# Norms as a factor on the projections' results: a transformer of six layers on one core

## The reference

```
y = x * rsqrt(mean(x * x) + EPS)            # one factor for each token
h = (y * g) * (1 + scale) + shift           # one factor and one addend for each channel
u, gate, q, k, v, ... = split(h @ w_in)
...
x = x + gate_of_layer * (mixed @ w_out)
```

## Time and profile before

| | us |
|---|---|
| median of 3 runs (lowest to highest) | 3006.55 (3005.95 to 3016.93) |
| the profiled execution, its own time | 3007.32 |
| its span, first to last instruction | 3005.5 |
| TensorE busy (matmuls) | 2804.0, 93% |
| VectorE busy | 1704.1, 57% |
| ScalarE busy | 938.5, 31% |
| GpSimd busy | 156.1, 5% |
| mean granted clock of TensorE | 0.963 |

### The profile page before, as it was taken

One profiled execution on the slowest core, in us unless ns is written; L12 is line 12 of the kernel. 1 busy time (PEld: TensorE's weight loads), 2 busy tenths in 40 slices (PEclk: granted clock), 3 DMA queues, 4 the chain that ended last, 5 costly groups with the idle time before them and its releaser, 6 DMA issues. The chain is left out here.

```text
span 3005.5 us, 36673 instructions
## 1 busy us (share of the span) xinstructions
PE 2804.0 (93%) x14298; PEld 2326.8 (77%) x14298; DVE 1704.1 (57%) x2637; ACT 938.5 (31%) x1440; POOL 156.1 (5%) x84
## 2 busy tenths in 40 slices
PE   7898999999999986998988999999999899999999
PEld 7777777877877875776866778888888677878887
DVE  3886666666577878785545455442333546554333
ACT  2212334444232221332334332122122335342222
POOL 0000000000000000000025200000000006200000
PEclk8999999999999998999998999999999999999999
DMA  5242343433245643432300024321222120122332
GB/s 205 91 141 92 99 140 119 137 125 126 93 157 185 194 128 118 135 109 78 123 4 1 25 82 141 119 92 63 64 63 64 48 85 1 38 82 91 98 92 97
DMA packets 88541, 296.33 MB, mean 99 GB/s; under 512 B 10289, under 2 KB 13361, under 8 KB 87857
## 3 DMA queue, kind: packets, MB, share of 16 engines
q1 hardware_dynamic: 88368, 293.98, 30.3%
HBM read 291.85 MB, written 2.10 MB: 98 GB/s over the span
## 5 line engine op out<-in xcount | busy, mean ns | idle before, releaser
L754 PE MATMUL turns<-h_hi,w_hi 128*128 128x512 f32 (+1 forms) x2480 | 800.7, 372 | 62.8 <-ACT u_padded L1124 31.9
L754 PE MATMUL turns<-h_hi,w_lo 128*128 128x512 f32 (+1 forms) x2480 | 780.3, 364 | 0.0
L754 PE MATMUL turns<-h_lo,w_hi 128*128 128x512 f32 (+1 forms) x2480 | 777.9, 363 | 0.0
L754 PEld LDWEIGHTS turns<-h_hi,w_hi 128*128 128x128 f32 x2480 | 424.6, 192 | 163.8 <-issue 64.8
L754 PEld LDWEIGHTS turns<-h_lo,w_hi 128*128 128x128 f32 x2480 | 422.0, 192 | 73.3 <-issue 1.0
L754 PEld LDWEIGHTS turns<-h_hi,w_lo 128*128 128x128 f32 x2480 | 420.6, 191 | 75.1
L1199 DVE TENSOR_TENSOR w_lo<-w_raw,w_hi 128x1024 fp32r<-128x1024 f32 x300 | 366.9, 1223 | 140.8 <-ACT w_hi L995 138.4
L995 ACT ACTIVATE w_hi<-w_raw 128x1024 fp32r<-128x1024 f32 x300 | 315.7, 1053 | 377.5 <-PE turns L754 354.7
L709 POOL TENSOR_SCALAR tmp<-tmp,softmax_stats 128x768 f32<-128x768 f32 (+1 forms) x80 | 155.9, 1951 | 2428.8 <-DVE softmax_stats L1427 2428.4
L1202 DVE SCALAR_TENSOR_TENSOR x_lat<-turns,modulation,x_lat 128x512 f32<-128x512 f32 x112 | 84.1, 751 | 336.9 <-PE turns L754 336.9
L754 PE MATMUL turns<-m_hi,w_lo 128*128 128x512 f32 (+1 forms) x768 | 233.2, 358 | 0.0
(11 more groups left out here) (212 smaller groups left out, 3405.2 us busy)
## 6 DMA issues: line engine op xcount, KB each, us to landing
w_raw<-in_wpack SPq DMA_DIRECT2D x300, 512.0 KB, 3.5
ada_raw<-in_adapack SPq DMA_DIRECT2D x176, 512.0 KB, 4.0
bias<-in_bias SPq DMA_DIRECT2D x64, 320.0 KB, 3.0
ada_first_a<-in_adapack SPq DMA_DIRECT2D x12, 512.0 KB, 8.7
x_lat<-in_xT SPq DMA_DIRECT2D x1, 2048.0 KB, 8.5
x_ctx<-in_ctxT SPq DMA_DIRECT2D x2, 1024.0 KB, 8.6
ada_first_b<-in_adapack SPq DMA_DIRECT2D x4, 512.0 KB, 14.7
cond_rows<-in_crow SPq DMA_DIRECT2D x4, 512.0 KB, 10.3
```

The lines of the kernel that those rows point to most:

```text
L754: ins = pe.matmul(dst[:, lo:lo + sz], w, x[:, lo:lo + sz], start=first and n == 0, stop=last and n == 2)
```

## The change

- Only the first norm is left as it was. In front of the others x is multiplied by the gain column alone (step `raw`: ScalarE writes `h_hi`, VectorE `h_lo`), which needs no statistics, so it happens while the last `xupd` units still run. If those units read `h` themselves (pooling layers and the attention part of the second block), a raw tile waits until the last unit is through with it (`h_free`).
- `nstat` and `back` move behind tiles 4 and 6 (7) of the joined pair; the squares are summed in a step `xsum` of their own. The result is copied to `inv_rms`. The `keep_warm` MATMULs of the norms go.
- `h_hi`/`h_lo` have two more columns in front, which hold the shifts. A projection unit multiplies them too and so gets W times shift. The 514 columns of a unit with T = 512 go as 258 + 256; with T = 768, as 512 + 258.
- Each such unit gets a step `rawz` on VectorE ahead of its eviction: copy the two shift columns of the result to `unit_shift`, multiply the rest by `inv_rms` into `unit_out`. The eviction then reads `unit_out` and adds the shift, on ScalarE in most cases. For `u` the shift is left out (the window mean takes off any constant), and VectorE writes `u_padded` itself.
- The norm between the blocks and the first norm of the second block become one: the sums of x squared and of (x final_g) squared are taken together. `x_lat` is multiplied by final_g and 1/rms later (`final`), among the units of the next layer.
- `w_lo` has two buffers where it had three: VectorE splits unit w+2 behind unit w, not w+3. TensorE waits for the second of a pair's weights and buffer only when it comes to it.

```diff
+    def raw_pair(n, u, v):
+        raws, nst, back = n
+        u.after, v.after, u.stats = list(raws), list(raws), (nst, back)
+        join(u, v)
...
-        Hh, Hl = sb("h_hi", [P, KT, TT], F32R), sb("h_lo", [P, KT, TT], F32R)
+        Hh, Hl = sb("h_hi", [P, KT, TT + 2], F32R), sb("h_lo", [P, KT, TT + 2], F32R)
...
-        Wh, Wl = sb("w_hi", [P, 3, D], F32R), sb("w_lo", [P, 3, D], F32R)
+        Wh, Wl = sb("w_hi", [P, 3, D], F32R), sb("w_lo", [P, 2, D], F32R)
...
+            def pieces_of(s):
+                if s.raw is None:
+                    return [(lo, lo, sz) for lo, sz in segs(s.T)]
+                return [(0, 0, TX), (TX, TX, TC + 2)] if s.T == TT else [(254, 0, 258), (TX, 258, 256)]
...
                 for j in range(len(ks) + lag):
+                    if s.stats is not None and j == 4:
+                        stat_sums(s.stats[0])
+                    if s.stats is not None and j == (7 if s.stats[0].final else 6):
+                        stat_back(s.stats[1])
+                    if v and j == lag:
+                        pe.wait_ge(w_split, v.w + 1)
+                        free_turn(v)
                     if j < len(ks):
                         tile(s, ks[j], j == 0, j == len(ks) - 1)
...
+                elif s.kind == "raw":
+                    take()
+                    for c, (lo, sz) in enumerate(segs(t)):
+                        ins = stt(Tl[:, s.k, lo:lo + sz], xseg(lo, s.k), GA[:, c, s.k:s.k + 1],
+                                  Th[:, s.k, lo:lo + sz].bitcast(F32), ALU.mult, ALU.subtract)
+                    done(ins)
...
+                elif s.kind == "rawz":
...
+                        shift = PS[:, b, o:o + 2]
+                        if f is None:
+                            dve.tensor_copy(BC[:, b, :], shift)
...
+                        done(tt(ZT[:, 0:t], x, RB[:, 0:t], ALU.mult))
...
+                    if s.raw and s.ev in ("gate", "cgate", "sk", "sq", "su", "sgv"):
+                        chain(shifted(ZT, s))
...
-                    split_unit(s.w + 3)
+                    split_unit(s.w + 2)
```

More of the change, by code:

```diff
@@ L77, in __init__ @@
         self.swap = False
+        self.raw, self.stats, self.frees, self.need, self.final = None, None, False, [], False
 ACT_ONLY, DVE_ONLY = {"u", "v", "cg", "sk", "sq", "sf"}, {"cv", "cb"}
+RAW_EV = {"u", "gate", "q", "k", "g", "v", "cg", "cv", "cb", "cgate", "sk", "sq", "sf", "su", "sgv", "mlp"}
 def ends_in(s):
     if s.kind in ("upart", "scores", "trans", "pvmm", "back", "cond_rows"):
+        return None
+    if s.kind == "unit" and s.ev == "u" and s.raw is not None:
         return None
@@ L183, in pool_layer @@
                 y.append(s)
-        for m in range(KT):
-            full("H", "xupd", T, m, after=y if m == 0 else (), sect=SECT0[L] + 2, nxT=nxT)
-    pool_layer(0, TT, TT)
-    tiles = norm(TT, 1, SECT0[1])
+        return updates("H", T, SECT0[L] + 2, nxT, after=y, nxt=nxt)
+    n = pool_layer(0, TT, TT, nxt=(1, SECT0[1], TT))
     seq = ["q", "k", "g", "v"]
@@ L290, in plan @@
         sect = SECT0[4 + L]
-        tiles = norm(TT, 4 + L, sect)
+        finals = []
         todo, rp = None, None
@@ L312, in plan @@
             if j < 2:
-                u = full("H", e, t, m, after=tiles, layer=L, what=e)
+                u = full("H", e, t, m, layer=L, what=e)
                 if j:
-                    join(sk, u)
+                    raw_pair(n, sk, u)
                 else:
@@ L324, in plan @@
                     vt = add("vtrans")
-                    vt.after = [v]
+                    vt.after = [v] + finals[-1:]
                 u = half_unit("H", e, t, 1, m=m, layer=L, what=e, pair=0)
                 with_ada(u)
+                if both and len(finals) < KT:
+                    finals += [add("final", k=len(finals) + j, T=TX) for j in range(2)]
             if e == "v":
@@ L461, in plan @@
             s.turn = turn
-        elif s.of is not None:
+        elif s.of is not None and s.kind not in ("raw", "rawz"):
+            s.turn = s.of.turn
+    for s in steps:
+        if s.kind == "rawz":
             s.turn = s.of.turn
@@ L466, in plan @@
     for s in steps:
-        n = {"hnorm": 0, "back": 0, "rope": 1, "vtrans": 1, "scores": s.st, "trans": 1 if s.na else None}.get(s.kind)
+        n = 1 if s.kind == "nstat" and s.raw else {"hnorm": 0, "back": 0, "rope": 1, "vtrans": 1, "scores": s.st, "trans": 1 if s.na else None}.get(s.kind)
         if n is not None:
@@ L603, in build_blocks @@
         first_ctx2 = [s for s in by_kind["sq0"] if s.x0 == TX][0]
-        na_norm_end = [s for s in by_kind["ntile"] if s.g == 1][-1]
+        freeing = [s for s in by_kind["unit"] if s.frees]
+        na_norm_end = [s for s in by_kind["raw"] if s.g == 1][-1]
         four_first = [s for s in by_kind["four1"] if s.m == 0 and s.n0 == 0]
@@ L827, in _ @@
                     ins.then_inc(turn_mm, 1)
+                elif s.kind in ("nstat", "back") and s.raw:
+                    pass
                 elif s.kind == "nstat":
-                    if s.g != 0:
-                        keep_warm(26 if s.g == 4 else 8)
                     pe.wait_ge(dve_done, s.d0)
@@ L1031, in _ @@
                 b = None if s.turn is None else s.turn % 2
-                ps = None if b is None else PS[:, b, :]
+                ps = None if b is None else ZT[:] if s.kind == "unit" and s.raw else PS[:, b, :]
                 t = s.T
@@ L1125, in _ @@
                         done(ins)
+                    elif s.ev == "g" and s.raw:
+                        chain(shifted(T1, s))
+                        give(act.activation(G2[:, s.pair % 2, :], T1[:, 0:t], ACT.Tanh, scale=0.5))
                     elif s.ev == "g":
```

321 lines of the change are left out of this document (222 added, 99 removed).

## The result

The change makes the kernel slower: 3039.8 us median of five runs (3031.1 to 3045.1) against 3009.3 (3006.0 to 3016.9) for the kernel before, ratio 1.0099 with an interval of [1.0075, 1.0123]. The forecast was 2960, between 2915 and 3003: the direction is wrong, and the size by 80 us.

The account below looks back on a forecast made before the run. TensorE was taken as the bound (busy 93% of the span); -133.2 + 17.7 + 16.8 + 15 + 5 + 48 - 17 = -47.7 us from 3007.3 gave about 2960 us, range 2915 to 3003.

Parts of the forecast that it names:

- Term 5: w_lo with two buffers: waits at the third unit behind a norm, nothing in the steady state; +5 us.
- term 6: VectorE's pass over each result and ScalarE's shift, in convolution, gates, attention and head norms, nothing in MLPs; +48 us.
- terms 1, 2 and 4: Seven norms: leaving the path -133.2 us, sums and transposes staying on TensorE +17.7, second unit of the pair delayed +15.
- term 7: Earlier split ends VectorE's waits for w_hi in u units: layer 0 -11 us, layer 3 -6, together -17.
- term 4: Pairs at norms: VectorE's queue at the last xupd frees the second unit's buffer late; +15 us, between 0 and 35.
- Term 3: Projection units: 2544 more matmuls at +0.0061 us each, plus two shift columns for 768 tokens; together +16.8 us.
- Rival D: Units with 512 tokens: halved matmuls are paced by their weight loads, slower, 3329 us; chance 0.04.
- A: VectorE's added work and delays hide better, half of terms 4 and 6: 2928 us; chance 0.17.
- B: Pairs at norms: statistics come too late for the first rawz, 4 us at seven places, 2988 us; chance 0.10.
- C: VectorE becomes the bound, 99 us of its added work lands on the path: 3010 us, no change; chance 0.14.
- E: New waits in conv, gates or layer 4 drop the clock: 2990 us, with C 3040; bad form's chance 0.05.

Follow-up runs that it names:

- early split: Changed kernel with the split of w_lo for unit w+2 moved right behind rawz of unit w, ahead of the remaining eviction and chunks; 2973.2 us, ratio 0.988.
- fair counterpart: Kernel before with two w_lo buffers, VectorE splitting w+2, not w+3, and ahead of the eviction for units that read h; 2944.1 us, ratio 0.977.
- third-buffer kernel: Changed kernel with the early split, three w_lo buffers and both units of a pair split behind the last xupd but one; 3003.0 us, ratio 0.997.

## Why the prediction was wrong, by its steps

**Term 5 failed.** It gave `w_lo` with two buffers 5 us, and the early split gives 67 back. The step that was wrong is that "in the steady state the same chain (4.5) fits into a unit's 5.6, so it costs nothing". I had timed mlp, whose VectorE is nearly free. The chain's length is not what matters, but what VectorE has queued by then: in conv rows it works 90 us of 106 in the stretch of the last four rows, with two chunk passes of 1.28 behind each split, in attention the softmax, in gates the window means. My own term 6 said so of these stages and term 5 did not use it. A slack of one unit was gone with the buffer, and the split took the last place in the eviction behind a longer chain. In the old kernel, with its shorter chain, the same late place of the split costs 18 us (2962.1 against 2944.1) where it costs 67 in the changed one, so it is the two together. What a third buffer would have given with the split left late, no run shows.

**Without it the forecast is nearly met, and that is in good part luck.** -47.7 less the 5 is -53; the early-split kernel is 37 below before. But against its fair counterpart the norms give 75, where terms 1, 2 and 4 had 100, and the rest costs 106, where terms 3 and 6 had 65. What makes up for both is the order of the splits: 65 us between the spans of the old kernel and the counterpart, where term 7 had 17. By stage, after and early split against before:

- *Terms 1, 2 and 4*, the norms: forecast -133.2 + 17.7 + 15, about -100; measured -78. The waits ahead of the second unit are there, 4.5, 0.6, 4.1, 4.3, 3.8, 0.3 and 2.7 us, 20.4 for my 15, and by the mechanism of term 4: the third-buffer kernel shows the queue in front of the last `xupd`. The rest of the 22 is clock. The rows above have 0.80 to 0.93 in five of seven stretches; length by what is missing to 1.00 makes 17 us, an estimate. I had priced the pairs at the full clock.
- *Term 3*: forecast +16.8; measured 18 (put into the old kernel) and 23 (taken out of the changed one). The size is right by two errors: each matmul costs 0.0133 and not 0.0061, but TensorE pays it in half of the places. The stream of 256 was a good stand-in (0.2386 for two, 0.240 measured). The stream of 512 was not: the earlier trace rows has products with `m`, 0.2333 apart, while those with `h`, which the change halves, start 0.2267 apart (87.04 us for 384). The Trainium skill, "TensorE: Matmul & The Clock Gate", section "Back-to-back issue gap", gave the estimates of 160 by its sustained spacings and 9 by the isolated gap; the runs are far from the first and double the second. Rival D is out.
- *Term 6*: forecast +48.
  - *Conv* +16: after has 32 in the rows and 4 in the x units behind. 19 go with the early split; of the 12.6 left, 8 rows of 1.28 are the halving, 10. VectorE's pass adds next to nothing to that, though VectorE is busy 87.7 us of 93.3 in the last four rows of the early-split kernel: a busy share is no proof of a bound. It isn't free either: without the halving TensorE waits for VectorE again, and the rows fall by 3.5 only. My reading of the old rows was a little long, too: a row is 21.8 us (87.04 / 4), and the cut of the earlier trace rows is wider than one.
  - *Gates* +11: measured +10.8, and yet wrong, since the early split brings them to 61.3, where they were.
  - *Attention* +13: measured +25; with the early split +5, but 23 above its fair counterpart, 3 us a pair.
  - *Head norms* +8: measured +28, with the early split still +25. That is the other large miss. Here the chain of `rawz`, shift, copy and square does end TensorE's wait, as my term said (below, before and early split), but the clock falls with it (0.89 in the row above, 0.96 in layer 5 before). Of the 34.5 over the fair counterpart the shift pass is 11 and the halving 3. Cut another way, the granted clock was 0.90 and 0.89 in the two layers against 0.96 and 0.94; length by what is missing to 1.00 makes 26 us against 10, so some 15 of the 34.5 are slow clock behind the waits, an estimate. What else lengthens the waits is open.
  - *MLP* 0: right once the split is early. TensorE waits nowhere in layer 5's MLP then; of the 9.3 left, taking the halving out gives 6.0 back (in the old kernel it cost 8.7), and the rest is the wider distance of the 512s.
- *Term 7*: forecast -17; the u units gave -10.1 and -3.2. The mechanism was right and its reach far too short: the order that made VectorE wait for `w_hi` cost the old kernel 55 us, in heads, attention and mixes too. I had the row with 1.9 us and looked for it in the u units alone, although the wait stands as 138.4 us in 146 places in the list of waits.

TensorE's waits for ScalarE's square ahead of the head sums in layer 5's heads, before and with the early split:

```profile
PE scores L851 <- ACT tmp L1158: 3.8, 1, 3.8
```

```profile
PE scores L943 <- ACT tmp L1282: 9.9, 4, 5.3
```

**The rivals.** None named the late split. A is out: the additions cost more than forecast, not less. B didn't occur: `inv_rms` was ready before the first `rawz` in all seven stretches, in six of them by 1.4 us or more; in the fourth it came 0.2 us ahead, and TensorE waited 0.9 us behind that pair. C and the bad form of E gave 3010 and 3040, and the second number is the result's, by accident: it contains C, and VectorE is not the bound (59% busy, 1792.8 us). The loss of clock that E described did come (0.963 to 0.948; in the heads 0.92 to 0.88 and 0.96 to 0.89). But the clock follows the waits, and the longest of the new ones were the split's: with the early split it is 0.957.

**What would have shown it**: MLP units above 5.75, which I had named (eight dense ones of layer 5 take 46.1 us, 5.77 each), and stages of term 6 that lose more than 50 us in sum (conv rows, gates, neighbourhood attention and heads lose 96). The wait for `w_lo` I had not named there.

## What to carry to other kernels

A buffer taken from a double-buffered stream is priced by the queue in front of the instruction that refills it, in the busiest stage, not by the length of the chain in a calm one; and it is first a question of order: put the refill ahead of whatever in that queue is not yet due. Before a change is judged by its total, ask which part of it is separable: here a reordering that came along was worth -49 us in the old kernel and a badly placed instruction +67 in the changed one, both larger than the 31 by which the change loses to its fair counterpart. And a wait that an off-path engine has in 146 places deserves a try of its own before any restructuring.

## What the runs showed that I had not expected

- Halving a matmul of 512 columns costs 13.3 ns per extra matmul in a dense stream of the old kernel: 256 + 256 starts 0.240 apart (92.16 us for 384 pairs), 512 alone 0.227. Between kernels and operands the distance of 512s is not the same: 0.227 for `h` before, 0.2315 for `h` in the changed kernel, 0.2333 for `m`.
- Two costs in one stage need not add: in the conv rows the halving and VectorE's longer work hide behind each other.
- The granted clock was raised by matmuls in the gaps (0.89 to 0.95) with no gain in time.
- The stretch up to the first pair took between 90 and 101 us, and layer 5's attention between 182 and 193, in a pattern that follows none of the changes.
